# Twenty of thirty-two late modulation vectors computed as VectorE row sums instead of TensorE matmuls, in a two-layer hybrid diffusion trunk

## The reference

```python
def _trunk_layer(x, p, l, cond, ctx):
    mod = (cond @ p['w_ada'][l] + p['b_ada'][l]).reshape(cond.shape[0], 1, 6, D_MODEL)
    sh_a, sc_a, gt_a, sh_m, sc_m, gt_m = [mod[:, :, i] for i in range(6)]
    h = _rmsnorm(x, p['norm_mix_w'][l]) * (1.0 + sc_a) + sh_a
    mix, new_ctx = _mixer_sublayer(h, p, l, ctx)
    x = x + gt_a * mix
    h = _rmsnorm(x, p['norm_mlp_w'][l]) * (1.0 + sc_m) + sh_m
    x = x + gt_m * (jnp.square(jax.nn.relu(h @ p['mlp_w1'][l])) @ p['mlp_w2'][l])
    return x, new_ctx
```

```python
    stacked = jnp.stack(branches, axis=2)
    proj = jnp.einsum('blnc,ncd->blnd', stacked, w_branch)
    gates = jax.nn.sigmoid(z_gate.reshape(bsz, seq, N_BRANCH, D_MODEL))
    return jnp.einsum('bld,de->ble', jnp.sum(gates * proj, axis=2), w_out)
```

## Time and profile before

| | us |
|---|---|
| median of 3 runs | 2723.34 (2722.84 to 2723.85) |
| the profiled execution | 2714.22 |
| its span in the profile | 2712.4 |
| TensorE busy | 2593.4 (96%) |
| VectorE busy | 1373.8 (51%) |
| ScalarE busy | 981.1 (36%) |
| GpSimd busy | 666.5 (25%) |
| gates in `attention`, layer 0 and 1 | about 452 to 757 and 1790 to 2094 |
| gates in `merge`, layer 0 and 1 | about 752 to 850 and 2089 to 2187 |
| TensorE's granted clock, mean | 0.993 |

### The profile page before, as it was taken

One profiled execution on the slowest core, in us unless ns is written; L12 is line 12 of the kernel. 1 busy time (PEld: TensorE's weight loads), 2 busy tenths in 40 slices (PEclk: granted clock), 3 DMA queues, 4 the chain that ended last, 5 costly groups with the idle time before them and its releaser, 6 DMA issues.

```text
span 2712.4 us, 55055 instructions
## 1 busy us (share of the span) xinstructions
PE 2593.4 (96%) x23766; PEld 2415.4 (89%) x23766; DVE 1373.8 (51%) x2295; ACT 981.1 (36%) x1590; POOL 666.5 (25%) x525
## 2 busy tenths in 40 slices
PE   5998999999999999999999989999999999999997
PEld 5887897889899999999988888888898998999997
DVE  5767624236633646255575775342464347364364
ACT  4251043334422534253341511443344226253352
POOL 2322122222233220211323311322222331211202
PEclk8999999999999999999999999999999999999999
DMA  8110012433343123222330100134332431122222
GB/s 347 40 55 3 3 59 87 142 107 104 108 131 128 63 92 111 83 97 102 131 132 32 48 4 11 62 120 130 99 115 100 143 105 63 63 86 79 74 83 78
DMA packets 73148, 245.38 MB, mean 90 GB/s; under 512 B 7828, under 2 KB 20276, under 8 KB 71888
## 3 DMA queue, kind: packets, MB, share of 16 engines
q1 hardware_dynamic: 69936, 218.21, 23.7%
q0 software_dynamic: 2976, 23.69, 2.4%
HBM read 224.66 MB, written 17.20 MB: 89 GB/s over the span
## 4 chain that ended last, share of the span: by engine, by line
PE 83%; DVE 6%; ACT 5%; issue 3%; DMA 1%; POOL 0%; SPq 0%; DVEq 0%; ACTq 0%; POOLq 0%
PE ps_dense L1027 29%; PE ps_dense L1035 17%; PE ps_dense L1890 5%; PE ps_aux L1027 4%; PE ps_dense L1657 3%; PE ps_dense L1894 3%; PE ps_aux L1421 2%; PE ps_dense L1735 1%; PE ps_aux L1657 1%; PE ps_aux L1711 1%; PE ps_dense L1061 1%; PE ps_aux L1407 1%; PE ps_dense L1723 1%; PE ps_aux L1373 1%; DMA arena<-in_w_early 1%
## 5 line engine op out<-in xcount | busy, mean ns | idle before, releaser
L857 POOL TENSOR_TENSOR w_low<-w_ring,w_high 128x256 fp32r<-128x256 f32 (+1 forms) x338 | 515.7, 1542 | 1450.6 <-ACT w_high L2050 1444.3
L2050 ACT ACTIVATE w_high<-w_ring 128x1024 fp32r<-128x1024 f32 x200 | 212.1, 1061 | 460.2 <-PE ps_dense L1027 260.5
L1027 PE MATMUL ps_dense<-z_both,w_high 128*128 128x320 f32 x2048 | 312.5, 310 | 0.0
L1027 PEld LDWEIGHTS ps_dense<-z_both,w_high 128*128 128x128 f32 x2048 | 302.6, 188 | 2.1 <-issue 1.6
L1035 PE MATMUL ps_dense<-h_high,w_high 128*128 128x320 f32 x1024 | 242.2, 318 | 7.1 <-DVE x_res L3043 3.1
L1035 PE MATMUL ps_dense<-h_high,w_low 128*128 128x320 f32 x1024 | 233.2, 309 | 0.0
L1035 PE MATMUL ps_dense<-h_low,w_high 128*128 128x320 f32 x1024 | 232.5, 308 | 0.0
L3187 DVE SCALAR_TENSOR_TENSOR x_res<-ps_dense,mod,x_res 128x320 f32<-128x320 f32 (+2 forms) x192 | 72.6, 434 | 292.2 <-PE ps_dense L1027 292.2
L1027 PE MATMUL ps_dense<-h_high,w_high 128*128 128x320 f32 x864 | 204.5, 318 | 14.8 <-ACT h_high L2091 11.4
L1027 PE MATMUL ps_dense<-h_low,w_high 128*128 128x320 f32 x864 | 186.8, 309 | 0.0
L1035 PEld LDWEIGHTS ps_dense<-h_high,w_high 128*128 128x128 f32 x1024 | 167.8, 188 | 14.5 <-issue 12.6
(11 more groups left out here) (528 smaller groups left out, 5084.5 us busy)
## 6 DMA issues: line engine op xcount, KB each, us to landing
w_ring<-in_w_mlp SPq DMA_DIRECT2D x128, 512.0 KB, 3.6
w_ring<-in_w_gate SPq DMA_DIRECT2D x64, 640.0 KB, 3.9
w_ring<-in_w_late SPq DMA_DIRECT2D x64, 512.0 KB, 4.9
w_ring<-in_w_in SPq DMA_DIRECT2D x48, 512.0 KB, 3.5
w_ring<-in_w_out SPq DMA_DIRECT2D x16, 512.0 KB, 3.5
w_ring<-in_w_early SPq DMA_DIRECT2D x16, 512.0 KB, 3.5
arena<-in_dft POOLq DMA_DIRECT2D x2, 2944.0 KB, 14.9
x_kept<-x_res POOLq DMA_DIRECT2D x2, 2560.0 KB, 11.9
```

Source lines behind the costliest of these rows:

```text
L857: last = g.tensor_tensor(w_low[:, n % 2, k:k + step], ring[:, slot, k:k + step, :], w_high[:, n % 2, k:k + step].bitcast(F32), ALU.subtract)
L1027: last = mm(out[:, s, 0:HALF], w_[:, par_, k, :], x_[:, k, s * HALF:(s + 1) * HALF], start=first, stop=final)
L2050: a(w_high[:, n % 2], ring[:, j, 0:KC, :], ACT.Copy).then_inc(w_high_in.sem, 1)
```

## The change

- 20 late blocks (1 to 10 and 22 to 31, those not in `BY_ROWS`) are no longer computed by TensorE. Their weights are stored turned, so that output channels lie on partitions and the 1024 input channels on the free axis. VectorE multiplies them by the condition, broadcast to all partitions, and sums along the row (`late`, scalar_tensor_tensor with accum_out): two instructions (640 and 384 columns, into the scratch `mt`) for the latents' condition, one of 1024 in place for the context's. In `attention` these are parts c = 1 and c = 3 of the block's own gate; in `merge` all three stand ahead of VectorE's wait for the tanh.
- The other 12 blocks (0 and 11 to 21) stay as they were.
- The condition goes to DRAM once (`cond_rows`), and in each layer a broadcast DMA of 2048 values to 128 partitions (`cond_all`) is issued by SyncE ahead of gate 1's load, into space of the tables that the rotations used. For this the tables and parameters become one tensor and are laid out anew, and the reload between the layers grows from 1536 columns to all from `tri` on. The parameters that are loaded first grow by `wab`.
- The projection's two tiles move from the gate block to the late block (`w_gate` 512 KB, `w_late` 640 KB). The gate block's slot is refilled as soon as GpSimd's low part has read it (`w_low_in`), not when the gate is done; the late block's slot after VectorE's `proj_used` where the previous block in it was summed by VectorE. `w_out`'s first four loads follow the same rule.
- In the last layer's MLP TensorE no longer waits for operand A22's low part ahead of the place where the next layer's early rows would stand.

The diff, cut to its core:

```diff
+BY_ROWS = (0, *range(11, N_FLOW))
-N_TURN = N_LATE + N_EARLY // PACK
+N_TURN = len(BY_ROWS) + N_EARLY // PACK
...
-CON_FIRST = CON["ident"][0]
-PAR_FIRST = PAR["wab"][0]
+CON_FIRST = CON["ident"][0]
+PAR_FIRST = PAR["uq"][0]
...
+        cond_all = tables[:, at_cond:at_cond + 2 * D]
-        reload = slice(at_s1, CON["rot"][0] + CON["rot"][1])
+        reload = slice(at_s1, CON_W)
...
                 for i in range(N_GATE):
-                    load(l, B_GATE + 2 * i, ins["w_gate"], slice(i, i + 1), 10)
-                    load(l, B_GATE + 2 * i + 1, ins["w_late"], slice(i, i + 1), KC)
+                    if i == 0 and l == 0:
+                        sp.wait_ge(residual.sem, 1)
+                        dst = cond_rows.rearrange("o (p k c) -> (o p) k c", c=2, k=KC)
+                        sp.dma_start(dst, cond_pad[:, :, 2 * PACK - 2:2 * PACK]).then_inc(cond_in.sem, 16)
+                    if i == 1:
+                        sp.wait_ge(cond_in.sem, 16 * (l + 2))
+                        sp.wait_ge(*rot_in.nth(l, 5))
+                        sp.dma_start(cond_all, cond_rows.partition_broadcast(P)).then_inc(cond_in.sem, 16)
+                    load(l, B_GATE + 2 * i, ins["w_gate"], slice(i, i + 1), KC,
+                         ready=w_low_in.nth(l, W_GATE + i - 1) if i >= 2 else None)
+                    if i >= 2 and i - 2 not in BY_ROWS:
+                        sp.wait_ge(*proj_used.nth(l, i - 1))
+                    load(l, B_GATE + 2 * i + 1, ins["w_late"], slice(i, i + 1), 10)
...
                 if c == 3:
-                    landed(l, B_GATE + 2 * i + 1)
-                    rows_of(late_rows, ring[:, (2 * i + 1) % RING]).then_inc(gate_ps.sem, 1)
+                    if i in BY_ROWS:
+                        landed(l, B_GATE + 2 * i + 1)
+                        last = rows_of(late_rows, ring[:, (2 * i + 1) % RING])
+                    last.then_inc(gate_ps.sem, 1)
                 if c == 4:
                     pe.wait_ge(*gate_act.nth(l, i + 1))
-                    turn_rows(l, late_at(1, i), i)
+                    if i in BY_ROWS:
+                        turn_rows(l, late_at(i), BY_ROWS.index(i))
                     projected(l, i, flow_out)
...
-                        split_tile(dense_banks(b), b, k, h_high, h_low)
-                    landed(l, B_GATE + 2 * i + 1)
-                    rows_of(tail_rows(b), ring[:, (2 * i + 1) % RING]).then_inc(gate_ps.sem, 1)
+                        last = split_tile(dense_banks(b), b, k, h_high, h_low)
+                    last.then_inc(gate_ps.sem, 1)
...
-                    turn_rows(l, late_at(1 - b, i), i)
...
-                    quadrant_pair(l, p, (lambda: early(i // 2)) if i % 2 == 0 and (g or i) else None)
+                    quadrant_pair(l, p, (lambda: early(i // 2)) if i % 2 == 0 and (g or i) and l + 1 < DEPTH else None)
...
+            def late(l, i, c):
+
+                place = B_GATE + 2 * i + 1
+                if i == 1 and c == 0:
+                    dve.wait_ge(cond_in.sem, 16 * (l + 3))
+                if c == 0:
+                    dve.wait_ge(ring_in[place % RING].sem, (l * PER_SLOT + (1 + place // RING + 1)) * 16)
+                w = ring[:, place % RING, 0:KC].rearrange("p k n -> p (k n)")
+                cond_c = cond_all.rearrange("p (k c) -> p c k", c=2)[:, c]
+                row = mod[:, N_EARLY + i, c:c + 1]
+                pieces = ((0, T, mt[:, 0:T], row), (T, D, mt[:, 0:D - T], late_rest[:, i:i + 1])) if c == 0 else ((0, D, w, row),)
+                for a, b, product, total in pieces:
+                    link(v.scalar_tensor_tensor(out=product, in0=w[:, a:b], scalar=1.0, in1=cond_c[:, a:b], op0=ALU.mult,
+                                                op1=ALU.mult, accum_out=total))
...
                 i, c = divmod(q, 5)
-                if c == 3:
+                if c in (1, 3) and i not in BY_ROWS:
+                    late(l, i, c // 2)
+                if c == 3 and i in BY_ROWS:
                     dve.wait_ge(*gate_act.nth(l, i + 1))
-                    keep_rows(late_rows, i)
+                    keep_rows(late_rows, BY_ROWS.index(i))
                 if c == 4:
+                    dve.wait_ge(*gate_act.nth(l, i + 1))
                     dve.wait_ge(*block_done.nth(l, B_GATE + 2 * i + 2))
...
                 for i in range(N_FLOW, N_GATE):
                     d, b = i % KC, i % 2
+                    for c in range(2):
+                        late(l, i, c)
                     dve.wait_ge(*gate_act.nth(l, i + 1))
-                    keep_rows(tail_rows(b), i)
```

More of the change, by code:

```diff
@@ L143 @@
 ROUND = 12582912.0
-DVE_LINKS = 195
+DVE_LINKS = 270
 ACT_LINKS = 23
@@ L744, in _, with load @@
             sp.dma_start(x[:], ins["x"]).then_inc(x_in.sem, 16)
-            def load(l, place, dram, at, subs, more=0):
-                sp.wait_ge(block_done.sem, l * N_BLOCKS + more + (N_EARLY + place + 1))
+            def load(l, place, dram, at, subs, more=0, ready=None):
+                sp.wait_ge(*(ready or (block_done.sem, l * N_BLOCKS + more + (N_EARLY + place + 1))))
                 src = dram[l, at].rearrange("o p (s m) -> p (o s) m", m=P)
@@ L825, in _ @@
                                 keys_load(1, T, KEYS, 0, 0, 4)
-                stream(l, B_OUT, 0, N_OUT, ins["w_out"], KC)
+                for j in range(RING):
+                    if j % 2:
+                        sp.wait_ge(*proj_used.nth(l, N_GATE - 1 + j // 2))
+                    load(l, B_OUT + j, ins["w_out"], slice(j, j + 1), KC,
+                         ready=None if j % 2 else w_low_in.nth(l, W_GATE + N_GATE - 1 + j // 2))
+                stream(l, B_OUT + RING, RING, N_OUT - RING, ins["w_out"], KC)
                 with sp.Fori(0, GROUPS) as g:
@@ L3053, in gate_sum @@
                     dve.wait_ge(*proj_used.nth(l, i + 1))
-                    v.tensor_tensor(x[:, i % KC], x[:, i % KC], mt, ALU.add)
+                    link(v.tensor_tensor(x[:, i % KC], x[:, i % KC], mt, ALU.add))
             def attention(l):
@@ L3601, in lay_out @@
     early = np.roll(w_ada[:, :N_EARLY], -1, axis=0)
-    arrays = {"const": con, "x": xs, "cond": cond, "w_early": early, "w_late": w_ada[:, N_EARLY:], "w_in": blocks(win_cols),
-              "w_gate": w_gate, "w_out": blocks(f["w_out"]), "w_mlp": w_mlp, "par": np.roll(par, -1, axis=0),
+    w_late = w_ada[:, N_EARLY:].reshape(DEPTH, N_LATE, P, KC * P).copy()
+    turned = w_ada[:, N_EARLY:].transpose(0, 1, 4, 2, 3).reshape(DEPTH, N_LATE, P, KC * P)
+    for i in range(N_LATE):
+        if i not in BY_ROWS:
+            w_late[:, i] = turned[:, i]
+    w_late = np.concatenate([w_late, wb.reshape(DEPTH, N_GATE, P, 2 * P)], 3)
+    arrays = {"const": con, "x": xs, "cond": cond, "w_early": early, "w_late": w_late, "w_in": blocks(win_cols),
+              "w_gate": wg, "w_out": blocks(f["w_out"]), "w_mlp": w_mlp, "par": np.roll(par, -1, axis=0),
               "dft": dft}
```

65 lines of the change are left out of this document (36 added, 29 removed).

## The result

The changed kernel takes 2683.55 us (median of 4 runs, 2679.14 to 2690.67), the kernel before on the same chip 2723.09 (4 runs, 2719.61 to 2723.85): a ratio of 0.9866, with a 95% interval of 0.9848 to 0.9884, or 39.5 us less. The forecast was 2702, in a range of 2686 to 2718. The direction is right, the gain is almost twice the forecast, and the median is 2.5 us under the range. The profiled execution took 2679.14, with a span of 2677.3 us: 35.1 under the span of before.

The account below looks back on a forecast made before the run. TensorE was taken to bound both stretches of gates. Per layer -9.0 (gates 1 to 10), -1.9 (22 to 24), 0 (25 to 31), +0.3 (broadcast); two layers -21.2, start +0.4, a load -0.3: 2723.3 - 21 = 2702 us, range 2686 to 2718.

Parts of the forecast that it names:

- What bounds the kernel: First attention's gates and `merge`: TensorE sets the pace, busy 15.00 of 15.00 us and 95.99 of 96.00.
- TensorE's share of a gate, 0.80: One merge gate: removing the rows returns 0.66 us and the turning 0.14, so 9.78 becomes 8.98.
- The row sums, 2.6 us with reads of 0.05: VectorE, per block: sums over 640, 384 and 1024 elements take 0.82 + 0.56 + 1.23 us, each sum read 0.05.
- Case 4: VectorE row sums take two cycles per element, 4.7 us a block; +9 us a layer, 2741 us; chance 10%.
- Gates 22 to 24, 1.9: Start of `merge`: gate 22 saves 0.3 us, gates 23 and 24 save 0.8 each, 1.9 a layer.
- Gates 25 to 31 give nothing: Rest of `merge`: VectorE and GpSimd exclude each other, so a gate takes 9.8 us against 9.78 and the 0.80 is lost.
- the one that waited gets the next turn: VectorE two-SBUF-input and GpSimd instructions exclude each other; the waiting engine goes next, from a 2.78 us tensor_tensor.
- Case 2: In `merge` sums and splits interleave free or GpSimd goes first; seven gates keep 0.8 us; 2691, or 2688; chance 22%.
- case 1: The forecast itself: merge gives nothing from gate 25 on; 2696 to 2712 us; chance 50%.
- The copy of the condition, 0.3 a layer: Broadcast on SP's queue ahead of gate 1's weights makes them land later; costs 0.3 us a layer, bounds 0 and 3.
- Loads, tables, the last layer's MLP: nothing but 0.3 in layer 1: Late and `w_out` loads, table reload and last MLP change nothing; a layer 1 late weight load saves 0.3 us.
- The signatures: Profile signs: VectorE's busy time rises over 90 us; wrong if `merge` falls to 9.0 a gate, among others.

## Why the forecast was right in its direction and short in size

- **What bounds the kernel:** right. TensorE set the pace in both stretches, and without sums and rows a merge gate is its 8.79.
- **TensorE's share of a gate, 0.80:** too small. It is 0.98 in the merge; the 0.66 and 0.14 were right (0.67 and 0.14), the 0.09 and 0.07 behind them were left out. In gates 1 to 10 it is 0.80 to 1.21, and gates 5 and 10 save 1.09 and 1.21 where 1.3 was worked out: 9.7 a layer against 9.0, with two errors of opposite sign in it.
- **The row sums, 2.6 us with reads of 0.05:** right (0.82, 0.56, 1.23, reads of 0.08). Case 4, the half rate of the Trainium skill (Vector Engine (DVE) Microarchitecture Reference, Points that are easy to get wrong), is refuted here: 1.23 us for 1024 columns with the sum, 1.226 for the sumless one of rows 7.
- **Gates 22 to 24, 1.9:** nearly right. Gates 23 and 24 save 0.98 each, not 0.8, and gate 22 0.1 to 0.2, not 0.3.
- **Gates 25 to 31 give nothing:** the step that failed, and 11.9 of the 14 us by which the spans miss the forecast lie in the merge (15.7 against 3.8). Its order of split, 1024 sum and low part came in one of the 14 gates, at 9.74. It took the order of one gate for that of all seven, and its rule "the one that waited gets the next turn" doesn't hold always: in gate 26 of layer 1 the sum waited for the low part as well. In the other 12 gates the split, some 0.02 to 0.08 us earlier, caught the 384 sum. In all 13 GpSimd's two instructions passed first, which is what TensorE needed. What fixes the order beyond that is open; that it costs 1.2 to 2.5 us a merge, and that the one edit to the split's phase ends it (87.34), is shown. Case 2 named this outcome ("GpSimd goes ahead of them") at 2688 to 2691, and the spans lie nearer to it than to case 1. Its 2688 is a slip: twice 0.3 for the broadcast from 2691 are 2690.
- **VectorE's next limit:** the forecast followed GpSimd's chain alone. From gate 29 on it is VectorE's own 9.15.
- **The copy of the condition, 0.3 a layer:** not settled. Gate 0's length follows the landing of the values' store: 1.0 shorter in layer 0, where this landing scatters with the copy or without, and 2.2 longer in layer 1, where the copy alone doesn't explain it.
- **Loads, tables, the last layer's MLP: nothing but 0.3 in layer 1.** Right within the noise: 0.9994 for all of them together, with 0.8 in the merge of layer 1. The start cost 0.2, not 0.4.
- **The signatures** "wrong if `merge` falls to 9.0 a gate" and "VectorE's busy time up by over 90": the first came true: eight gates of the merge took 8.77 to 9.17 us in layer 1. The second rose by 166, of which some 60 are sums standing still.

## What to carry to other kernels

When work is taken off the bounding engine, read the hand-over from the timeline on both sides: the first instructions behind a removed one of another shape get faster too (0.16 of 0.98 us here). Where two engines exclude each other, the order can hang on hundredths of a microsecond, so don't forecast seven gates from one; ask rather what fixes the phase, and move that (a DMA issue in front of GpSimd's split was worth 1.2 to 2.5 us a merge). Compare more than one gate and more than one layer before a rule is made of an order. Work given to an engine with room costs nothing only behind the instruction that others wait for: the same sums gave nothing ahead of the row maximum and 6.9 us a layer behind it.

## What was unexpected of the hardware

A VectorE sum caught near its end by a GpSimd instruction lasts as long as all of GpSimd's that are queued: 0.56 us of work took 3.98 behind 2.40 and 0.73, and 4.13 behind three. One that waits from its start is mostly let in between two of them, but not always: 3.37 and 4.08 us in the same gate of two layers. A cast of 640 columns, with a single SBUF input, was held as well (2.58 for 0.49), as the section named above says can happen to casts. A 128 KB store landed 1.99 us after its issue in one kernel and 4.00 in another, with the same transfers ahead of it at the same distances.
